# QKV projections of the stick-breaking and MoBA layers in three rounded passes, and one ScalarE table for exp and log

## The reference, cut to what matters

```python
def stick_breaking_attention(x, w_qkv, w_o):          # moba_attention begins alike
    q, k, v = (to_heads(t) for t in jnp.split(x @ w_qkv, 3, axis=-1))   # 1024 -> 3 x 1024, 16 heads of 64
    ...
    z = einsum('bhqd,bhkd->bhqk', qb, k) * scale
    log_keep = where(past, -softplus(z), 0.0)
    tail = cumsum(log_keep, axis=3, reverse=True) - log_keep
    w = where(past, exp(log_sigmoid(z) + tail), 0.0)
    return einsum('bhqk,bhkd->bhqd', w, v)
```

## Time and profile before

| | us |
|---|---|
| median of 3 runs | 4002.61 (3992.7 to 4003.91) |
| the profiled execution, its own time | 3990.7 |
| its span | 3988.9 |
| busy: PE, DVE, ACT, POOL | 3781.0, 2164.1, 1555.0, 1101.1 |
| mean granted TensorE clock | 0.975 |

### The profile page before, as it was taken

One profiled execution on the slowest core, in us unless ns is written; L12 is line 12 of the kernel. 1 busy time (PEld: TensorE's weight loads), 2 busy tenths in 40 slices (PEclk: granted clock), 3 DMA queues, 4 the chain that ended last, 5 costly groups with the idle time before them and its releaser, 6 DMA issues.

```text
span 3988.9 us, 46662 instructions
## 1 busy us (share of the span) xinstructions
PE 3781.0 (95%) x17679; PEld 2987.0 (75%) x17679; DVE 2164.1 (54%) x2221; ACT 1555.0 (39%) x1935; POOL 1101.1 (28%) x574
## 2 busy tenths in 40 slices
PE   8999999999999899999999998998999998998899
PEld 6865888767888668886588786687777786686787
DVE  5644766426665356664466545336655545437554
ACT  4355444334433344344543332234343332234343
POOL 6700848305657018481065001030000001031000
PEclk9999999999999999999999999998999999998999
DMA  8634767446766157674376453201465453302463
GB/s 269 228 100 149 246 211 251 150 127 212 252 206 222 45 191 252 201 248 125 102 253 200 154 172 102 100 30 54 168 199 180 159 168 101 115 14 77 157 199 126
DMA packets 493256, 649.69 MB, mean 163 GB/s; under 512 B 16075, under 2 KB 393442, under 8 KB 493090
## 3 DMA queue, kind: packets, MB, share of 16 engines
q1 hardware_dynamic: 472356, 569.62, 44.3%
q0 software_dynamic: 19584, 75.50, 5.4%
q10 hardware_dynamic: 1150, 2.29, 0.2%
HBM read 646.29 MB, written 1.05 MB: 162 GB/s over the span
## 4 chain that ended last, share of the span: by engine, by line
issue 59%; POOLq 19%; PE 13%; POOL 7%; SPq 1%; ACT 1%; DMA 0%; DVE 0%; DVEq 0%; ACTq 0%
POOLq L602 7%; POOLq L604 6%; POOLq L606 5%; PE bank L1287 3%; PE bank L932 3%; POOL mod_zone L609 2%; POOL modrow L609 2%; PE bank L904 1%; PE bank L1423 1%; PE bank L1434 1%; POOL modrow L591 1%; POOL mod_zone L591 1%; PE bank L911 1%; PE bank L912 1%; PE bank L913 1%
## 5 line engine op out<-in xcount | busy, mean ns | idle before, releaser
L2141 DVE TENSOR_TENSOR wproj_lo<-wproj,wproj_hi 128x2048 fp32r<-128x2048 f32 x252 | 756.9, 3040 | 132.7 <-ACT wproj_hi L1671 132.7
L932 PE MATMUL bank<-wproj_hi,x_hi 128*128 128x512 f32 x2112 | 541.2, 398 | 21.8 <-DVE arena L2232 12.1
L932 PE MATMUL bank<-wproj_lo,x_hi 128*128 128x512 f32 x2112 | 534.4, 396 | 0.0
L932 PE MATMUL bank<-wproj_hi,x_lo 128*128 128x512 f32 x2112 | 526.3, 392 | 0.0
L1711 ACT CAST actT_hi<-bank 128x512 fp32r<-128x512 f32 x132 | 77.4, 587 | 1074.6 <-PE bank L959 1074.6
L932 PEld LDWEIGHTS bank<-wproj_hi,x_hi 128*128 128x128 f32 x2112 | 396.5, 190 | 117.6 <-issue 29.8
L566 POOL TENSOR_SCALAR rstd<-sumsq 128x1 f32<-128x1 f32 x38 | 7.5, 197 | 1704.9 <-ACT tok L1654 1704.7
L1671 ACT CAST wproj_hi<-wproj 128x2048 fp32r<-128x2048 f32 x252 | 469.9, 1911 | 14.5 <-DMA wproj<-in_ffn_w_gate_up 14.5
L932 PEld LDWEIGHTS bank<-wproj_hi,x_lo 128*128 128x128 f32 x2112 | 400.5, 190 | 84.7
L932 PEld LDWEIGHTS bank<-wproj_lo,x_hi 128*128 128x128 f32 x2112 | 387.6, 188 | 76.6
L904 PE MATMUL bank<-wproj,xT 128*128 128x384 f32 (+2 forms) x1216 | 421.3, 502 | 8.2 <-issue 4.7
(11 more groups left out here) (431 smaller groups left out, 5182.7 us busy)
## 6 DMA issues: line engine op xcount, KB each, us to landing
wproj<-in_ffn_w_gate_up SPq DMA_DIRECT2D x336, 512.0 KB, 6.0
wdown<-in_ffn_w_down SPq DMA_DIRECT2D x132, 1024.0 KB, 5.0
wproj<-in_ffn_w_gate SPq DMA_DIRECT2D x84, 512.0 KB, 5.0
wproj<-in_ffn_w_up SPq DMA_DIRECT2D x84, 512.0 KB, 6.6
wproj<-in_w_in SPq DMA_DIRECT2D x40, 1024.0 KB, 7.3
mod_zone<-in_mod_w POOLq DMA_DIRECT2D x36, 1024.0 KB, 6.9
modrow<-in_mod_w POOLq DMA_DIRECT2D x36, 1024.0 KB, 6.9
wproj<-in_sb_w_qkv SPq DMA_DIRECT2D x48, 512.0 KB, 5.3
```

Of the source, the lines that this page charges most:

```text
L932: last = nc.tensor.matmul(proj_ps[t][:, :], rounded(x_part[of_x](c)[:, toks]), rounded(w_part[of_w][:, c, :]), start=start and c == 0, sto ...
L2141: V.tensor_tensor(rounded(wproj_lo[w.odd][:, cols]), src[:, cols], wproj_hi[w.odd][:, cols], ALU.subtract).then_inc(cols_lo, 1)
```

## The change: rounded passes, their parts, and the table

1. For sb and MoBA, `project_in_halves` replaces `project`: for each half of the tokens 8 products of high x and high weights, 8 of low x and high weights, 8 of high x and low weights, all rounded, 384 columns.
2. x is split at the entry of these mixers as it is for an FFN: `enter_mix` with `pair_x_hi_parts`, and `squares` on ScalarE calls `round_x` before each `square`. The high part of x lies in the unused columns of `wproj_hi`.
3. ScalarE makes the high part of a pair's weights in two casts of 128x1536 (`round_pair`). The first two pairs are cast in the last two FFN steps, pair k+2 in iteration k: in sb the first cast stands between `softplus_tails` and `evac`, the second behind `exp_arg` of head 0; in MoBA the first behind both `weights`, the second behind `copy_outputs`.
4. The low part is made over the raw weights in two subtractions of 128x1536: by VectorE for the first two pairs of a layer and for all of MoBA (`rest_of_pair`, ahead of `prepare`), by GpSimd for pairs 2 to 7 of sb (`rest_of_pairs`).
5. SP loads a pair in six transfers of 256 KB, the first four chunks of q, k, v and then the other four (`heads_in_halves`).
6. ScalarE loads the table set that has exp and log (`natural_log_exp_and_others`) once ahead of an sb layer's attention and in `rwkv` and `hgrn`; the dummy Exp is gone.

```diff
+            def project_in_halves(i, w, t, mid):
+                k = i.s - n.pair
+                ...
+                if k == 0:
+                    pe.wait_ge(x_rounded, 4 * n.entries + 2 * (t + 1))
+                for c in range(KC):
+                    if t == 0 and c % BC == 0:
+                        pe.wait_ge(pair_hi, 2 * (n.split + k) + 1 + c // BC)
+                    if mid is not None and c == BC:
+                        mid()
+                    nc.tensor.matmul(proj_ps[t][:, 0:384], rounded(pair_x_hi(c)[:, toks]), rounded(hi[:, c, :]), ...)
+                if k == 0:
+                    x_here(t)
+                for c in range(KC):
+                    nc.tensor.matmul(proj_ps[t][:, 0:384], rounded(x_lo[:, c, toks]), rounded(hi[:, c, :]), ...)
+                for c in range(KC):
+                    if t == 0 and c % BC == 0:
+                        weights_rest(c // BC)        # pair_lo_vector or pair_lo
+                    last = nc.tensor.matmul(proj_ps[t][:, 0:384], rounded(pair_x_hi(c)[:, toks]), rounded(lo[:, c, :]), ...)
+                last.then_inc(proj_done, 1)
...
+            def rest_of_pairs():                     # GpSimd, sb layers
+                for k in range(2, N_PAIRS):
+                    slot = (n.load + k) % 2
+                    for half in range(2):
+                        cols = pair_half(half)
+                        pool.wait_ge(pair_hi, 2 * (n.split + k) + 1 + half)
+                        nc.gpsimd.tensor_tensor(rounded(wproj_lo[slot][:, cols]), wproj[slot][:, cols],
+                                                wproj_hi[slot][:, cols], ALU.subtract).then_inc(pair_lo, 1)
...
+            def round_pair(i, w, parts=range(2)):    # ScalarE
+                for half in parts:
+                    act.wait_ge(pair_in[w.odd][half], i.half(3 * DMA, 3 * DMA))
+                    cols = pair_half(half)
+                    nc.scalar.copy(rounded(wproj_hi[w.odd][:, cols]), wproj[w.odd][:, cols]).then_inc(pair_hi, 1)
...
                     if k + 2 < FF_STEPS or k + 2 == FF_STEPS and ffn_next:
                         round_columns(st.plus(2), w.plus(2))
+                    if k + 2 >= FF_STEPS and pairs_next:
+                        round_pair(Step(n.split + k + 2 - FF_STEPS), w.plus(2))
...
                     for hd in range(2):
                         nc.scalar.activation(soft[:, hd], soft[:, hd], ACT.Ln, bias=1.0).then_inc(sb_soft, 1)
-                    nc.scalar.activation(table_pick[:, :], minus_half[:, 0:1], ACT.Exp)
...
                         softplus_tails(i, u)
+                        if ahead_pair:
+                            round_pair(split_pair, w.plus(2), [0])
                         if more:
                             evac(i.plus(1), w.plus(1), 0)
                         if k:
                             copy_outputs(i.plus(-1), c.plus(-1))
                         exp_arg(i, u, 0)
+                        if ahead_pair:
+                            round_pair(split_pair, w.plus(2), [1])
                         if more:
                             evac(i.plus(1), w.plus(1), 1)
...
+                if kind == "sb":
+                    nc.scalar.preload_act_table_set("natural_log_exp_and_others")
...
+            def rest_of_pair(i, w):                  # VectorE
+                for half in range(2):
+                    cols = pair_half(half)
+                    v.wait_ge(pair_hi, i.n(2, 1 + half))
+                    V.tensor_tensor(rounded(wproj_lo[w.odd][:, cols]), wproj[w.odd][:, cols], wproj_hi[w.odd][:, cols],
+                                    ALU.subtract).then_inc(pair_lo_vector, 1)
...
+                        if kind == "moba" and k + 2 < pairs:
+                            rest_of_pair(Step(n.split - pairs + 2 + i.s - n.pair, i.j), Step(n.load + 2 + i.s - n.pair, i.j))
                         if k + ahead < pairs:
                             prepare(i.plus(ahead))
```

More of the change, by code:

```diff
@@ L153, in __init__ @@
         self.rows = 0
+        self.entries = 0
+        self.split = 0
     def dmas(self, w, per):
@@ L335, in x_hi, with pair_x_hi, pair_half @@
             return x_hi_parts[c // BC][:, c % BC, :]
+        pair_x_hi_parts = [wproj_hi[i][:, PAIR_COLS:KC * 512].rearrange("p (c s) -> p c s", s=SEQ) for i in range(2)]
+        def pair_x_hi(c):
+            return pair_x_hi_parts[c // BC][:, c % BC, :]
+        def pair_half(half):
+            return slice(half * PAIR_COLS // 2, (half + 1) * PAIR_COLS // 2)
         gate = sb("gate", [P, NT, 512])
@@ L408, in program @@
         cols_hi, cols_lo = sem("cols_hi"), sem("cols_lo")
+        pair_in = [[sem(f"pair_in{odd}_{half}") for half in range(2)] for odd in range(2)]
+        pair_hi, pair_lo_vector, pair_lo = sem("pair_hi"), sem("pair_lo_vector"), sem("pair_lo")
         rows_rounded, rows_lo = sem("rows_hi"), sem("rows_lo")
@@ L625, in _ @@
                     inverse_rms((0, 2, MLA_Q_RANK), (2, 4, MLA_KV_RANK))
+                    n.load += len(MLA_BLOCKS)
+                elif l % 3 == 0:
+                    rest_of_pairs()
+                else:
+                    n.split += N_PAIRS
+                n.load += N_PAIRS + len(WO_BLOCKS) + FF_STEPS
                 inverse_rms_rows()
@@ L729, in heads, with heads_in_halves, load @@
                 n.load += pairs
+            def heads_in_halves(w_qkv):
+                def load(i, w):
+                    room(w)
+                    dst = wproj[w.odd][:, 0:PAIR_COLS].rearrange("p (c s n) -> p c s n", c=KC, s=3)
+                    src = w_qkv.rearrange("(c p) (s n) -> p c s n", p=P, s=3)
+                    for half in range(2):
+                        chunks = slice(half * BC, (half + 1) * BC)
+                        for s in range(3):
+                            sp.dma_start(dst[:, chunks, s], src[:, chunks, s, bass.ds(i.n(P), P)]
+                                         ).then_inc(pair_in[w.odd][half], DMA)
+                run_steps(sp, N_PAIRS, 0, 0, lambda k, j: load(Step(k, j), Step(n.load + k, j)))
+                n.load += N_PAIRS
             def heads_mla(w_uq, w_ukv):
@@ L990, in ffn @@
                 gate_up(Step(n.ffn), Step(n.load), 1, entering=True)
-                n.ffns += 1
+                n.entries += 1
                 if 0 in rows:
@@ L1037, in attend @@
                 heads_cat = kind == "mla"
+                in_halves = kind in ("sb", "moba")
                 dk = MLA_QH if heads_cat else DH
@@ L1151, in out_chunks @@
                     if t == 0:
-                        pe.wait_ge(w_in[w.odd], DMA * (n.landed[w.odd] + (2 if kind == "mla" else 3) * pairs // 2 + 2))
+                        pe.wait_ge(w_in[w.odd], DMA * (n.landed[w.odd] + (2 if kind == "mla" else 0) * pairs // 2 + 2))
                     rhs = wproj[w.odd][:, :].rearrange("p (c n) -> p c n", c=KC)
@@ L1238, in attend @@
                 n.pair += pairs
-                n.loaded(pairs, 2 if kind == "mla" else 3)
+                n.loaded(pairs, {"mla": 2, "diff": 3}.get(kind, 0))
+                if in_halves:
+                    n.entries += 1
+                    n.split += pairs
                 if kind == "diff":
@@ L1804, in pair @@
                     more = k != pairs - 1
+                    ahead_pair = k + 2 < pairs and kind in ("sb", "moba")
+                    split_pair = Step(n.split + i.s - n.pair + 2, i.j)
                     if kind == "sb":
                         softplus_tails(i, u)
+                        if ahead_pair:
+                            round_pair(split_pair, w.plus(2), [0])
                         if more:
@@ L1846, in attend @@
                 n.load += pairs
+                if kind in ("sb", "moba"):
+                    n.split += pairs
                 if kind == "sb":
@@ L2147, in rest_of_rows, with take_x @@
                                 ALU.subtract).then_inc(rows_lo, 1)
-            def take_x(t, gain, split):
+            def take_x(t, gain, hi_parts=None):
                 scale, bias = gain
@@ L2166, in take_x @@
                                                    ALU.mult, ALU.add)
-                    last.then_inc(x_full if split else x_split, 1)
-                if split:
+                    last.then_inc(x_full if hi_parts else x_split, 1)
+                if hi_parts:
                     for h in range(2):
@@ L2201, in enter_mix @@
                     n.rstd += 1
-                take_x(t, gain, False)
+                take_x(t, gain, pair_x_hi_parts if split else None)
             def copy_even(kc, gain=None, bias=None, dst=xT):
@@ L2217, in copy_even, with ffn @@
                 n.odd += (kc + 1) // 2 // 2
-            def ffn(ffn_next, then, row=None, rows={}, layer=None, behind={}, begun=None):
+            def ffn(ffn_next, then, row=None, rows={}, layer=None, behind={}, begun=None, pairs_next=False):
                 scaled = row is not None
@@ L2243, in step @@
                         rest_of_columns(st.plus(2), w.plus(2))
```

(2 more changed lines are left out.)

68 lines of the change are left out of this document (50 added, 18 removed).

## The result

The changed kernel takes 4006.82 us (median of 20 runs) against 3992.62 (20 runs) for the kernel before: ratio 1.0031, 95% interval 1.0023 to 1.0039, or 12 us slower. The forecast was 9 us less: 3994, counted from the median of 4002.61 that three runs had given. The profiled executions have spans of 4007.5 and 3988.9 us.

What follows compares the result with a forecast made beforehand. TensorE, busy 95% of the span, was taken as the bound almost everywhere. MoBA -13.5, sb -8.5, entries +8.4, tables -1 and clock +6 gave -8.6, say -9 us: from 4002.6 to 3994, own range 3983 to 4004.

Steps and rivals of the forecast that it cites:

- Parts 1 and 2: Projections: 0.173 us per rounded 384-column pass, 2.1 us less a pair; cast 1.43 to 1.48, subtraction VectorE 1.71 to 1.75, GpSimd 3.50.
- Part 3: MoBA pairs: projection saves 2.1 us, the late second cast and subtraction give back 0.2; 7 pairs, taken as -13.5 us.
- Part 5: sb pairs: GpSimd's subtraction blocks VectorE's product for the first head's weights; period +15.4 us, -4.3 a layer, -8.5 for two.
- Part 6: Three entries from FFN to mixer: first pair's late load delays the last `down` by 4.0 us; net +2.8 each, +8.4.
- Part 7: The rest: one table for hgrn and rwkv -1 us (bounds 0, -5); TensorE's clock drops +6 (bounds 0 and +20).
- The other order at the door: sb pairs: first head's product gets in before GpSimd, second head's weights come 7 us late; 4016 us, chance 20%.
- sb is free: sb pairs: the collision of GpSimd and VectorE falls where nobody waits; 3968 us, chance 15%.
- the entries cost nothing: Entries from FFN to mixer: the first pair's first half lands early enough; 3982 us, chance 9%.

## Why the prediction was wrong, step by step

**Parts 1 and 2 were right.** Eight rounded records of 384 columns take 1.39 us, 0.173 each; a cast 1.47 (forecast 1.43 to 1.48), VectorE's subtraction 1.76 (1.71 to 1.75), GpSimd's first of a pair 3.48 (3.50), its second, begun beside L2496, 3.9.

**Part 3, MoBA, was right on the steady pair, and by luck on the total.** 13.28 us a pair for 13.3. The six periods together take 79.45 us for 93.13, that is -13.7 for -13.5, but the first of them gave 3.9, not 1.9: before it took 17.17, with a stretch at a granted clock of 0.81. After, the slow stretch (0.53) lies ahead of the first turn, and from the first projection to there it takes 26.3 us for 26.0, where the forecast had some 3 less.

**Part 5's mechanism was right and its size wrong.** L2496 lasts 3.85 us with L637 just ahead of it, in the order forecast. From the first turn of probabilities to the output projection the forecast has about -3 us a layer (five pairs by -0.3 and the last by -1.3, rounded up), and +4.3 and +3.4 were measured. The six full pairs have a mean of 16.35 us, over the 16 that the forecast had named as a sign of being wrong. The runs put the difference on the clock: with TensorE kept busy the pairs take 15.2 us (forecast 15.4; the added products fill a wait of about their own length) and that stretch is 4.7 and 3.0 us shorter than before; without it the waits of 2.19 and 0.94 us are followed by a pair at a granted clock of 0.66 that takes 19.6. I had read half of this in the earlier trace rows and priced it apart, as +6 for the whole kernel.

**Part 6's waits at the entries were nearly right, and its sum was not.** TensorE waits 5.21, 3.98 and 4.97 us for the last turn, 14.2 in all where I had 12. Until the first projection the entries lengthened by 26.3 us; of the 12.1 beyond the waits 11.7 are the same work behind the turn at granted clocks of 0.71 to 0.77. From the first projection to the first turn of probabilities an sb layer was to save 2.2 us (twice 2.1, less 0.9 for the second token tile and 1.1 for the first collision) and saved 0.5: the tile's wait is 0.78, but the first collision's is 2.16.

**Part 7 held the failed term.** The clock was +6 with bounds to +20. It is 12 at the entries and about 14 in sb (twice the 7 between the forecast's -3 and the mean of +4.3 and +3.4), some 26 together, outside the bounds. The sb share is a difference from the forecast, not a reading; the fill took 15.4 us off the same two stretches. The other term erred on the opposite side: the tables outside sb were -1, bounds to -5, and all loads together gave -12 on the kernel before (7 to 16), of which the forecast has 3.6. I took loads "mostly beside other engines" without following each to TensorE: three of them cost 3.3 us in one stretch of the last layer. Where some 5 of the 12 us lie no run shows.

**The sum again.** The stages of the two profiles (from the turn of step 9 to the output projection) give +13.2 in layer 0, -5.9 in layer 1 and +12.3 in layer 3, together +19.6 of the 18.6 us between the spans. The rest of the first stack gives +6.2 and the last layers -7.3. These two can't be put down to causes: the same last layers take 1752 to 1769 us in the twelve profiles (from 2200 us on), 1756 and 1769 in the two with the old tables. So the sum explains the direction and the stages, and not the last few us of the +12 (9 to 16).

**The rivals.** "The other order at the door" had nearly the right time, 4016, and is wrong as a cause: the first product, not the second head's, was blocked. "sb is free" and "the entries cost nothing" were wrong for this kernel; both are what one small edit each brings about, at -35 to -40 us and -27 us against after, where I had -26 and -12 against the forecast.

## What to carry to other kernels

Work added for a side engine goes behind what the bounding engine waits for in the side engine's queue, not where its data might first be there: here a cast that waited 5.60 us for its load stood ahead of a cast that TensorE needed, and moving it and its subtraction behind gave 27 us. Price a wait of the bounding engine with the slow stretch behind it, stall and clock as one term; rows at either level show the factor. A load costs what isn't covered of it: the same table loads cost 12 us with pairs of 15.67 us and 26 with pairs of 13.71.

## What the runs showed of the hardware beyond what was expected

- Added matmuls that fill TensorE's waits more than pay for themselves: about 20 us of them in the sb layers, and the kernel is 12 us faster; 12 us in the entries, and it is 8 us faster.
- The same code in the same stretch runs at one of two clocks from execution to execution: some 400 matmuls of the last layers take 75.1 us in four of the twelve profiles and 66.4 to 67.8 in eight.
- Waits of 2.19 and 0.94 us cost more in clock than in waiting: the pair behind them takes 19.57 us, where pairs with the same collision and TensorE kept busy take 15.2.
- Cutting GpSimd's instruction in four cuts the longest exclusion from 3.85 to 1.38 us and raises its total: 9.83 us for eight quarters against 6.9 for two whole ones, with VectorE's instructions of two SBUF inputs beside them longer by 0.6 to 0.8.
